# Gates, branch projections and most of a down projection with tokens on partitions

## What is computed

```
h = x + mixer(rms_norm(x))
# in the mixer: z = u @ w_in (2048 x 11264) -> hgrn2 (8 heads of 128), banded attention (16 heads of 64), gates (2 x 2048)
merged = sigmoid(gate_a) * (y_a @ w_branch_a) + sigmoid(gate_b) * (y_b @ w_branch_b)
mixer  = merged @ w_out
h = h + square(relu(rms_norm(h) @ w_up)) @ w_down       # 2048 -> 8192 -> 2048
x = rms_norm(h)
```

## Time and profile before

| what | us |
|---|---|
| median of three runs (2780.02 to 2781.06) | 2780.59 |
| profiled execution, its own time | 2781.22 |
| its span, first to last instruction | 2779.4 |
| TensorE matmul busy | 2765.6 |
| VectorE busy | 2075.5 |
| ScalarE busy | 1472.1 |

### The profile page before, as it was taken

One profiled execution on the slowest core, in us unless ns is written; L12 is line 12 of the kernel. 1 busy time (PEld: TensorE's weight loads), 2 busy tenths in 40 slices (PEclk: granted clock), 3 DMA queues, 4 the chain that ended last, 5 costly groups with the idle time before them and its releaser, 6 DMA issues.

```text
span 2779.4 us, 40598 instructions
## 1 busy us (share of the span) xinstructions
PE 2765.6 (100%) x15440; PEld 2377.4 (86%) x15440; DVE 2075.5 (75%) x3194; ACT 1472.1 (53%) x2184; POOL 63.6 (2%) x72
## 2 busy tenths in 40 slices
PE   9999999999999999999999999999999999999998
PEld 6888888888888888888888888888888888888887
DVE  5687888887677777777786677778778777777776
ACT  5456555565444444444465555556555555555554
POOL 0000000000000000000050000000000000000000
PEclk9999999999999999999999999999999999999999
DMA  7555555555555655555655655655565555555554
GB/s 266 189 172 166 187 173 174 172 190 189 181 193 190 193 184 189 190 191 188 210 197 188 195 180 169 196 175 188 184 203 190 183 192 191 192 190 190 190 189 144
DMA packets 157154, 521.98 MB, mean 188 GB/s; under 512 B 28960, under 2 KB 31392, under 8 KB 156704
## 3 DMA queue, kind: packets, MB, share of 16 engines
q1 hardware_dynamic: 155952, 517.31, 56.5%
q10 hardware_dynamic: 1008, 2.08, 0.2%
HBM read 517.22 MB, written 2.10 MB: 187 GB/s over the span
## 4 chain that ended last, share of the span: by engine, by line
PE 100%; DMA 0%; DVE 0%; ACT 0%; issue 0%; DVEq 0%; SPq 0%
PE acc L432 39%; PE acc L437 19%; PE psT L432 5%; PE psX L432 5%; PE acc_first L432 5%; PE psX L437 3%; PE psT L437 3%; PE acc_first L437 2%; PE acc L469 1%; PE acc L471 1%; PE acc L470 1%; PE psT L715 1%; PE psE L715 1%; PE psE L716 1%; PE psX L717 1%; PE psA L717 1%
## 5 line engine op out<-in xcount | busy, mean ns | idle before, releaser
L1216 DVE TENSOR_TENSOR w_lo<-w_raw,w_hi 128x1024 fp32r<-128x1024 f32 x958 | 1170.3, 1228 | 344.5 <-ACT w_hi L799 315.4
L799 ACT ACTIVATE w_hi<-w_raw 128x1024 fp32r<-128x1024 f32 x958 | 1003.0, 1055 | 553.0 <-PE acc L432 280.3
L432 PE MATMUL acc<-XU,w_hi 128*128 128x512 f32 x2848 | 930.6, 398 | 0.0
L437 PEld LDWEIGHTS acc<-XU,w_lo 128*128 128x128 f32 x2848 | 535.3, 188 | 122.5
L432 PE MATMUL acc<-XY,w_hi 128*128 128x512 f32 x1792 | 576.8, 397 | 0.0
L437 PE MATMUL acc<-XU,w_lo 128*128 128x256 f32 x2848 | 560.0, 278 | 0.0
L432 PEld LDWEIGHTS acc<-XU,w_hi 128*128 128x128 f32 x2848 | 447.8, 189 | 4.1 <-issue 2.7
L437 PEld LDWEIGHTS acc<-XY,w_lo 128*128 128x128 f32 x1792 | 336.7, 188 | 78.3
L437 PE MATMUL acc<-XY,w_lo 128*128 128x256 f32 x1792 | 352.4, 278 | 0.0
L432 PEld LDWEIGHTS acc<-XY,w_hi 128*128 128x128 f32 x1792 | 277.9, 189 | 5.5 <-DVE work L1222 2.7
L804 ACT ACTIVATE cross<-acc 128x256 f32<-128x256 f32 x242 | 92.5, 382 | 335.2 <-PE acc L432 335.2
(11 more groups left out here) (345 smaller groups left out, 3275.9 us busy)
## 6 DMA issues: line engine op xcount, KB each, us to landing
w_raw<-in_weights SPq DMA_DIRECT2D x962, 512.0 KB, 3.4
bias<-in_rel_bias SPq DMA_DIRECT2D x8, 384.0 KB, 3.9
bias<-in_rpb_back SPq DMA_DIRECT2D x32, 96.0 KB, 6.7
hT<-in_x_t SPq DMA_DIRECT2D x8, 256.0 KB, 7.5
G<-in_norm_rows SPq DMA_DIRECT2D x2, 1024.0 KB, 7.3
G<-in_pair_masks ACTq DMA_DIRECT2D x1, 960.0 KB, 5.1
out_dram<-G SPq DMA_DIRECT2D x2, 384.0 KB, 2.5
out_dram<-G ACTq DMA_DIRECT2D x2, 384.0 KB, 3.2
```

Of the source, the lines that this page charges most:

```text
L432: return nc.tensor.matmul(bank[:, :], hi[:, k, col:col + P], X[:, k0 + k, :], start=first and k == 0, stop=last and k == nk - 1 and k % 2 ...
L437: return nc.tensor.matmul(bank[:, 0:T], lo[:, k, col:col + P], X[:, k0 + k, 0:T], start=False, stop=last and k == nk - 1 and k % 2 == 0, s ...
L799: act.activation(w_hi[s][:, 0:n], w_raw[s][:, 0:n], ACT.Copy).then_inc(hi_done, 1)
L1216: V.tensor_tensor(w_lo[s][:, 0:n], w_raw[s][:, 0:n], w_hi[s][:, 0:n].bitcast(F32), ALU.subtract).then_inc(lo_ready, 1)
```

## The change

The gate projections of both mixers, their branch projections, and the down projection of the first feed-forward (but for its last group of eight contraction tiles) take the layout with tokens on partitions.

- **Gates.** Steps 10 to 17 of a head (6 to 13 in `heads2`) are eight `token_block`s into the banks `acc_first` and `acc[0]`. At step 0 of the next head, behind its rounding, ScalarE takes both banks out through Sigmoid, scaled by a column of the norm; TensorE waits for that ahead of step 2 of that head, which writes `acc[0]`. The gates' sums and scalings on VectorE and copies on ScalarE fall away. The head's own tiles alternate between `acc[1]` and `acc[0]`.
- **Branches.** Four chunks of 512 features, each four `token_block`s for either branch. VectorE multiplies by the gates and adds, TensorE turns the chunk back with eight transposes (`turn_chunk`) behind step 2 of the next chunk, ScalarE and VectorE split it. The last chunk is turned in `out1`/`out2` behind their second block, and the first four blocks there have another order (`out_order`).
- **Down projection.** 112 of 128 blocks become `token_downs`, taken out every four blocks by `chunk_out`. In `ffn1last` each of the 16 feature tiles begins with two transposes of that sum into its bank, and `products` of the last group adds to it. Up tiles have three banks in place of four.

Weight blocks keep their size and number; their content follows the layout.

```diff
+CHUNKS = D // CHUNK
+NEAR_TILES = {"heads1": 5, "heads2": 3}
+HEAD_CHUNK = 2 * P
...
+def out_order(i, b):
+
+    if i == 0 and b < 4:
+        return b % 2, b // 2
+    return b // 2, b % 2
...
-    plan = [("vals1", 1, 32, 0, 0, None), ("heads1", HEADS, 18, 9, 9, None), ("branch1", 2, 16, 16, 16, None), ("out1", 2, 16, 8, 0, None),
+    plan = [("vals1", 1, 32, 0, 0, None), ("heads1", HEADS, 18, 5, 5, None), ("branch1", CHUNKS, 2 * KB // 2, 0, 0, None), ("out1", 2, 16, 8, 0, None),
...
+            ("gmv", 1, 32, 0, 0, None), ("heads2", HEADS, 14, 3, 3, None),
+            ("branch2", CHUNKS, 2 * KB // 2, 0, 0, None), ("out2", 2, 16, 8, 0, None),
...
-        def head2_bank(i, t):
-            return acc[(7 * i + t) % 2]
+        def head_bank(t):
+            return acc[(t + 1) % 2]
...
         def ffn_bank(p, i, t):
-            if p.name.startswith("ffn2"):
-                return up_banks[(p.tile(i, t) - ph["ffn2first"].tbase) % 3]
-            shift = -ffn_counts(p.name)[1] % 4 if p.name.endswith("first") else 0
-            return four_banks[(t + shift) % 4]
+            if p.name == "ffn1last":
+                return last_banks[t % 4]
+            return up_banks[(p.tile(i, t) - ph[p.name[:4] + "first"].tbase) % 3]
 
         up_banks = [acc[0], acc[1], acc_first]
...
+        gate_banks = [acc_first, acc[0]]
+        branch_banks = [[psT, psX], [acc[1], psA]]
+        turn_banks = [[acc[0], acc_first], [psE, psS]]
...
+            def token_block(p, i, b, X, k0, banks, first, last):
+
+                s = p.slot(i, b)
+                hi = w_hi[s][:, :].rearrange("p (k n) -> p k n", k=2)
+                lo = w_lo[s][:, :].rearrange("p (k n) -> p k n", k=2)
+                pe.wait_ge(lo_ready, p.block(i, b) - RAW + 1)
+                for k in range(2):
+                    for a in range(NT):
+                        bank = banks[a]
+                        x_hi, x_lo = (X[:, k0 + k, T * n + a * P:T * n + (a + 1) * P] for n in range(2))
+                        nc.tensor.matmul(bank[:, :], x_hi, hi[:, k, :], start=first and k == 0, stop=False, skip_group_check=True)
+                        nc.tensor.matmul(bank[:, :], x_hi, lo[:, k, :], start=False, stop=False, skip_group_check=True)
+                        done = nc.tensor.matmul(bank[:, :], x_lo, hi[:, k, :], start=False, stop=last and k == 1, skip_group_check=True)
+                done.then_inc(w_used, 1)
+
...
+                near = NEAR_TILES[p.name]
                 for b in range(p.blocks):
                     t = b // 2
-                    if b % 2 == 0:
-                        bank_free(p, i, t)
+                    if t < near and b % 2 == 0:
+                        if t == 0:
+                            pe.wait_ge(acc_free, p.tile(i, 0) + TILE_CREDIT)
+                        else:
+                            bank_free(p, i, t)
+                        if t == 1:
...
+                    if t < near:
+                        products(p, i, b, head_bank(t), X, KB * (b % 2), b % 2 == 0, b % 2 == 1)
+                    else:
+                        if t == near and b % 2 == 0:
+                            pe.wait_ge(acc_free, p.tile(i, near - 2) + 1 + TILE_CREDIT)
+                        k0 = 2 * (b - 2 * near)
+                        token_block(p, i, b, X, k0, gate_banks, k0 == 0, k0 == KD - 2)
...
+            def turn_chunk(x, c):
+
+                pe.wait_ge(S(f"mixed{x}"), NT * (c + 1))
+                if c >= 2:
+                    pe.wait_ge(S(f"m_ready{x}"), 2 * (c - 1))
+                for n in range(2):
+                    bank = turn_banks[c % 2][n]
+                    for j in range(2):
+                        for a in range(NT):
+                            done = nc.tensor.transpose(bank[:, (2 * j + a) * P:(2 * j + a + 1) * P],
+                                                       G[:, 8 * c + 4 * n + 2 * a, j * P:(j + 1) * P], ident[:, :])
+                    done.then_inc(S(f"m_turned{x}"), 1)
 
...
+                p, x = ph[name], name[-1]
+                X = XY if name == "branch1" else XU
+                heads = ph["heads" + x]
+                pe.wait_ge(S(f"ya_ready{x}"), HEADS - 1)
+                for c in range(p.iters):
+                    for b in range(p.blocks):
+                        kind, k0 = b // 4, 2 * b
+                        if b % 4 == 0 and c:
+                            pe.wait_ge(S(f"branch_read{x}"), NT * (2 * c - 1 + kind))
+                        if c == 0 and b == 3:
+                            pe.wait_ge(S(f"ya_ready{x}"), HEADS)
+                        if c == 0 and b == 4:
+                            pe.wait_ge(S(f"yb_ready{x}"), HEADS)
+                            pe.wait_ge(acc_free, heads.tile(HEADS, 0) + TILE_CREDIT)
+                        token_block(p, c, b, X, k0, branch_banks[kind], b % 4 == 0, b % 4 == 3)
+                        if b == 2 and c:
+                            if c == 1:
+                                pe.wait_ge(S(f"gates_ready{x}"), NT * HEADS)
+                            turn_chunk(x, c - 1)
+
+            def out_projection(name):
...
+                        t, half = out_order(i, b)
+                        if half == 0:
+                            bank_free(p, i, t)
...
+                            pe.wait_ge(S(f"m_ready{x}"), 2 * (CHUNKS - 1))
+                        if i == 0 and b == 1:
+                            pe.wait_ge(S(f"branch_read{x}"), NT * 2 * CHUNKS)
+                        products(p, i, b, acc[t % 2], X, KB * half, half == 0, half == 1,
+                                 operand=mixed if i == 0 and b in (0, 2) else None)
+                        if i == 0 and b == 1:
+                            turn_chunk(x, CHUNKS - 1)
...
+                    ffn_bank_free(p, i, tile)
+                    if s.t % 4 == 0:
+                        pe.wait_ge(S("down1_out"), NT * (CHUNKS * (FF1 // KB - 2) + s.t // 4 + 1))
+                    bank = ffn_bank(p, i, tile)
+                    for a in range(NT):
+                        nc.tensor.matmul(bank[:, a * P:(a + 1) * P], feature_part(a, s.t // 4)[:, s.t % 4 * P:(s.t % 4 + 1) * P], ident[:, :],
+                                         start=a == 0, stop=False, is_transpose=True, skip_group_check=True)
+                    products(p, i, b, bank, A, ring_half(s.group, 0), False, True)
+                    tile += 1
...
+            def sigmoid_gates(x, i):
+                p, scales = ph[f"heads{x}"], mix_rs if x == 1 else tok_rs
+                act.wait_ge(w_used, p.block(i, p.blocks - 1) + 1)
+                for a in range(NT):
+                    act.activation(head_gates(i, a), gate_banks[a][:, :], ACT.Sigmoid, scale=scales[:, a:a + 1])\
+                       .then_inc(S(f"gates_ready{x}"), 1)
...
                     if b == 0:
                         round_next(p, i, b)
+                        if i:
+                            sigmoid_gates(1, i - 1)
                     if b % 2:
 
-                        copy_cross(p, i, t, b, acc_first if t == 0 else acc[(t - 1) % 2])
+                        if t < NEAR_TILES["heads1"]:
+                            copy_cross(p, i, t, b, head_bank(t))
                         round_next(p, i, b)
...
+            def mixed_high(x, c, X):
+
+                for n in range(2):
+                    j = 4 * c + 2 * n
+                    act.wait_ge(S(f"m_turned{x}"), 2 * c + n + 1)
+                    act.activation(X[:, j:j + 2, 0:T], turn_tiles(c, n), ACT.Copy).then_inc(S(f"mh_ready{x}"), 1)
...
+                sigmoid_gates(x, HEADS - 1)
+                for c in range(p.iters):
                     for b in range(p.blocks):
-                        round_block(p, i, b)
-                        gate = G[:, ds(gate_of(i, b), 1), :]
...
+                        if b == 3 and c:
+                            mixed_high(x, c - 1, X)
...
                     round_next(p, i, b)
+                    if b == 0 and i:
+                        sigmoid_gates(2, i - 1)
...
-                    if b in (11, 13, 15, 17):
-                        n = (b - 11) // 2
-                        tile_sum(p, i, 5 + n, b, 5 + n, bank, wk(8))
-                        ins = V.tensor_tensor(G[:, ds(i * 4 + n, 1), :], work[:, 8:9, 0:T],
-                                              rs[:, :].rearrange("p (a t) -> p a t", a=1), ALU.mult)
-                        if n == 3:
-                            mark(ins, S("gates_z1"), i + 1)
-                        else:
-                            link(ins)
...
+            def mixed_low(x, c, X):
+
+                for n in range(2):
+                    j = 4 * c + 2 * n
+                    dve.wait_ge(S(f"mh_ready{x}"), 2 * c + n + 1)
+                    mark(V.tensor_tensor(X[:, j:j + 2, T:2 * T], turn_tiles(c, n), X[:, j:j + 2, 0:T].bitcast(F32), ALU.subtract),
+                         S(f"m_ready{x}"), 2 * c + n + 1)
+
+            def gated(x, p, c, kind):
+
```

(58 more changed lines are left out.)

157 lines of the change are left out of this document (64 added, 93 removed).

## The result

The changed kernel takes 2814.68 us (median of 4 runs, 2813.68 to 2814.98) against 2780.61: ratio 1.0122, 95% interval 1.011 to 1.0135. It is slower, as forecast, but by 34 us and not by 20, and outside the range of 2794 to 2812.

What follows compares the result with a forecast made beforehand. The prediction took TensorE to bound the kernel: -20.4 for blocks, +10.6 for transposes, +21.5 and +8.3 for stalls in `heads1` and `heads2` gave +20.0 on 2780.6, so 2800.6 us. Forecast 2796 to 2803, range 2794 to 2812.

Steps and rivals of the forecast that it cites:

- What bounds it: Whole kernel: TensorE, busy 2765.6 of 2779.4 us, bounds it; a wait put in front of it costs its full length.
- which wait appears: Before step 2, TensorE waits for ScalarE's gate sigmoids: 3.1 us a head in `heads1`, 1.2 in `heads2`, seven heads each.
- The late load of the third head: In `heads2`, third head: rounding waits for its load from memory; 2.0 us more if it recurs, left to the range.
- The term of 0.06 for the semaphore: Before step 2: about 0.06 us from the end of ScalarE's sigmoids to TensorE's start, added in both mixers' waits.
- another table load: Step 1 in `heads2`: Gelu may need one, 1.28 us on ScalarE, hidden by four rounded blocks; otherwise 10 us.
- The clock: Whole kernel: the granted clock was expected to stay at 1.00, so the sum held no cost for a fall.
- rival 2: Stalls in `heads1` bring TensorE's clock down, 2.6 us each, 18 us more: 2819 us; chance 0.10.
- a sign that it is wrong: In the profile after: a falling clock was one of the listed observations that would make the prediction wrong.
- A block in either layout: Gates, branches, down projection: 0.067 us saved a block with tokens on partitions, 304 blocks, 20.4 us saved.
- Transposes: Turning branch chunks and down-projection tiles back on TensorE: 96 transposes at 0.11 us, 10.6 us added.
- A table load's drain: ScalarE before the sigmoids: the skill page's drain of about 1.38 us was judged absent; with it, 19 us longer, 2820.
- rival 4: ScalarE stops about 1.28 us around a table load between a rounding and a PSUM read; 18 us more, 2819; chance 0.02.

Runs made afterwards that it cites:

- vector_takes_gates: Changed kernel, but VectorE takes the gate banks out behind the same head's attention low part, with Sigmoid in the branch stage; 2774.60 us, ratio 0.9977.
- fill_the_wait: Changed kernel with 13 unused matmuls of 128x512 on TensorE ahead of the wait before step 2 in `heads1`; 2805.24 us, ratio 1.0087.
- sigmoid_at_last_step: Changed kernel with the two gate sigmoids at the last step of the same head, ahead of the attention's high part; 2785.58 us, ratio 1.0017.
- sigmoid_before_rounding: Changed kernel with the two gate sigmoids ahead of ScalarE's rounding at step 0, in both mixers; 2793.42 us, ratio 1.0046.
- longer_wait_heads2: Changed kernel with three more sigmoids of the first gate bank ahead of the two in `heads2` only; 2840.07 us, ratio 1.0214.

## Why the prediction was right in direction and wrong on the clock

- **What bounds it, and which wait appears.** Right. The wait was forecast at 3.1 us in `heads1` and 1.2 in `heads2`; it is 3.15 and 1.21, together 30.7 against 29.8. The late load of the third head came again but added 0.20 us, not 2.0. The term of 0.06 for the semaphore was an estimate; here it is 0.10. Gelu needed another table load in every head of `heads2`, which stayed hidden.
- **The clock: the step that failed.** The sum took the granted clock to stay at 1.00, so it had nothing for it; rival 2 ("the stalls bring TensorE's clock down") had a chance of 0.10 and is what happened, and the prediction had named a falling clock as a sign that it is wrong. I argued against it from the earlier trace rows: 4.4 us without a matmul at the end of the kernel, granted clock still 1.00. The profile after shows why that doesn't follow. In its six falls the record goes down 2.4 to 4.4 us after TensorE's last matmul ahead of the wait has ended, and in five of them only once TensorE is at work again. So a record that is still at 1.00 after 4.4 us of idle time says nothing on the clock that the next matmuls will get. The price of rival 2 was too high, though: 1.3 to 1.6 us a fall and not 2.6, six falls, 9.0 us. Here the lower level holds for some 3.4 us after each fall (287.0 to 290.4), where at the kernel's start it held for the first 5 us of matmuls.
- **A block in either layout.** 0.067 us held wherever blocks follow each other: -7.33 for 112 down blocks (forecast 7.5), +1.5 for each pair of branch and output stage (forecast 3.5 - 2.1 = 1.4). It did not hold in the heads. In the changed kernel, waits and clock taken off, they save 2.3 and 3.8 us in place of 4.3 each (2.0 in `heads1` of `vector_takes_gates`, 451.86 to 449.82). Of the gate steps of `heads1` only 15 and 16 save 0.067; 10, 12, 13, 14 and 17 save 0.02 to 0.05, and 11 takes 0.03 more. In step 11 the scan's product starts 0.32 us behind the block's last matmul, in steps 10 and 13 0.23; why, no run tells.
- **Transposes.** 0.11 us each, right: `ffn1last` +3.47 for 32 (3.5).
- **A table load's drain** (the Trainium skill, "ScalarE: Activation LUTs", section "What ACT_TABLE_LOAD costs", puts it at about 1.38 us): the load stands 0.02 us behind the rounding and the first Sigmoid 0.02 behind the load, so the gap of rival 4 is not there.
- **The other page.** The warning of the Trainium skill, "TensorE: Matmul & The Clock Gate", section "HAM oscillation — how this bites in real kernels", which I had set aside, was right that idle gaps between matmuls bring the lower clock; here it fell behind six of the seven waits of 3.15 us and not behind every one.
- **Small costs left out.** The first block behind a wait takes 0.08 to 0.09 us more without any change of the clock, 1.2 us in 14 heads.

Sum: waits 30.7, the slower first block 1.2, clock 9.0, layout and transposes -6.9: +34.0, against +34.1 measured. Of the 14 us that the forecast missed, 9.0 are the clock, 2.5 the smaller saving in the heads, 2.1 waits and first blocks.

## What to carry to other kernels

When an operand's drain moves to another engine, place it by that engine's program and not by its busy share: ScalarE is idle half the time here, and yet its one serial chain at the end of a head decides. The same change with the drain on VectorE, in a gap it already had, and Sigmoid in a stage with room, is 0.23% faster than before in place of 1.2% slower. Price a wait of TensorE at its length and at what the clock may cost behind it. In this kernel that was nothing behind 1.2 and 1.6 us; 2.2 us cost another 1.6 us in 2 of 7 cases, and 3.15 us or more another 1.3 to 1.6 us in 18 of 21.

## What the runs showed of the hardware

How often the clock fell behind a wait of this length, in runs of otherwise full load:

| wait, us | times | clock fell |
|---|---|---|
| 1.2 (1.4 once) | 14 | 0 |
| 1.6 | 7 | 0 |
| 2.2 | 7 | 2 |
| 3.15 | 14 | 12 |
| 3.4 to 3.6 | 7 | 6 |

(1.2: `heads2` of the changed kernel and of `fill_the_wait`; 1.6: `sigmoid_at_last_step`; 2.2: `sigmoid_before_rounding`; 3.15: `heads1` of the changed kernel and of `longer_wait_heads2`; 3.4 to 3.6: `heads2` of the latter.) Of the 20 falls, 18 came 0.1 to 1.5 us after TensorE had begun again and two 0.4 and 0.6 us before. The profile's busy digits don't show them: in the stretch at half the clock, 287.00 to 290.40, TensorE counts as busy for 3.40 of 3.40 us.
